# A recurrence's preparation of the next pair of heads, rearranged over the engines of one Trainium2 core

## The reference, cut to what matters

```python
xl = p_in + (shifted - p_in) * mu
r, k, v, xw, xa, xg = jnp.split(xl, RWKV_SPLITS, axis=-1)
w = -jax.nn.softplus(-(w0 + jnp.tanh(xw) @ w2)) - 0.5
decay = jnp.exp(-jnp.exp(w.astype(jnp.float32)))
a = jax.nn.sigmoid(a0 + xa @ a2)
kk = k * k_k
kk = kk / jnp.maximum(jnp.sqrt(jnp.sum(kk * kk, axis=-1, keepdims=True)), 1e-12)
k = k * (1.0 + (a - 1.0) * k_a)
# per token, with a_t = -kk and b_t = kk * a
sa = jnp.einsum('bhij,bhj->bhi', state, a_t)
state = state * w_t[:, :, None, :] + sa[..., None] * b_t[:, :, None, :] + v_t[..., None] * k_t[:, :, None, :]
y_t = jnp.einsum('bhij,bhj->bhi', state, r_t)
# behind the scan: group norm of y, then
y = y + jnp.sum(r * k * r_k, axis=-1, keepdims=True) * v
```

## Time and profile before

| | us |
|---|---|
| median of 3 runs | 2117.4 (2117.34 to 2122.9) |
| the profiled execution's own time | 2115.69 |
| its span, first to last instruction | 2113.9 |
| PE busy | 1930.1 (91%) |
| DVE, ACT, POOL busy | 875.9, 443.6, 1275.4 |
| mean granted clock of PE | 0.952 |

### The profile page before, as it was taken

The page is one execution under the profiler, slowest core; times in us unless marked ns, Lnnn a source line. Parts: engine busy times, 40 slices in busy tenths (PEclk is TensorE's granted clock), DMA queues, the critical chain, the costliest instruction groups (busy, mean ns, idle before and its releaser), DMA issues.

```text
span 2113.9 us, 29843 instructions
## 1 busy us (share of the span) xinstructions
PE 1930.1 (91%) x11700; PEld 1500.4 (71%) x11700; DVE 875.9 (41%) x1440; ACT 443.6 (21%) x876; POOL 1275.4 (60%) x615
## 2 busy tenths in 40 slices
PE   7999999878989999998899999967667899999998
PEld 5888888656658888886677766655565678888887
DVE  4333311468553333212223344384546735555301
ACT  3000000313430000001222356325423021112100
POOL 6888877553348888777465432351132667777773
PEclk9999999989989999999999999988876999999999
DMA  4222233211012222333323421310022223223231
GB/s 146 98 89 98 88 91 91 99 53 47 31 60 90 89 99 88 91 92 112 148 85 125 155 67 44 130 36 2 3 107 90 70 82 98 90 91 96 87 96 58
DMA packets 58780, 180.33 MB, mean 85 GB/s; under 512 B 6931, under 2 KB 13843, under 8 KB 58172
## 3 DMA queue, kind: packets, MB, share of 16 engines
q1 hardware_dynamic: 49132, 165.83, 23.5%
q10 hardware_dynamic: 9552, 13.13, 1.7%
HBM read 165.81 MB, written 13.13 MB: 85 GB/s over the span
## 4 chain that ended last, share of the span: by engine, by line
PE 80%; DVE 14%; ACT 3%; issue 2%; DMA 0%; ACTq 0%; POOL 0%; DVEq 0%; SPq 0%; POOLq 0%
PE bank L522 23%; PE bank L523 22%; PE bank L524 22%; PE bank L884 1%; PE bank L572 1%; PE bank L837 1%; DVE h_lo L1619 1%; PE bank L870 1%; DVE sq L2154 1%; PE bank L801 1%; DVE m_lo L2155 1%; PE bank L1040 1%; DVE xT L1666 1%; DVE tmp L1663 1%; DVE sq L2151 1%
## 5 line engine op out<-in xcount | busy, mean ns | idle before, releaser
L442 POOL TENSOR_TENSOR w_hi<-w_raw,one 128x1024 fp32r<-128x1024 f32 (+1 forms) x279 | 527.4, 1890 | 610.1 <-PE bank L524 600.1
L444 POOL TENSOR_TENSOR w_lo<-w_raw,w_hi 128x1024 fp32r<-128x1024 f32 (+1 forms) x279 | 698.9, 2505 | 21.9
L522 PE MATMUL bank<-h_hi,w_hi 128*128 128x512 f32 x1528 | 629.8, 412 | 25.1 <-DVE h_lo L1619 12.5
L523 PE MATMUL bank<-h_lo,w_hi 128*128 128x512 f32 x1528 | 608.8, 398 | 0.0
L524 PE MATMUL bank<-h_hi,w_lo 128*128 128x512 f32 x1528 | 608.5, 398 | 0.0
L522 PEld LDWEIGHTS bank<-h_hi,w_hi 128*128 128x128 f32 x1528 | 289.9, 190 | 119.2 <-issue 29.2
L523 PEld LDWEIGHTS bank<-h_lo,w_hi 128*128 128x128 f32 x1528 | 290.1, 190 | 76.6 <-issue 9.8
L524 PEld LDWEIGHTS bank<-h_hi,w_lo 128*128 128x128 f32 x1528 | 289.8, 190 | 70.8
L522 PE MATMUL bank<-a_hi,w_hi 128*128 128x512 f32 x528 | 209.3, 396 | 0.0
L523 PE MATMUL bank<-a_lo,w_hi 128*128 128x512 f32 x528 | 209.3, 396 | 0.0
L524 PE MATMUL bank<-a_hi,w_lo 128*128 128x512 f32 x528 | 209.3, 396 | 0.0
(11 more groups left out here) (345 smaller groups left out, 2177.6 us busy)
## 6 DMA issues: line engine op xcount, KB each, us to landing
w_raw<-w_ffn_gu_dram SPq DMA_DIRECT2D x88, 512.0 KB, 3.4
w_raw<-w_conv_up_dram SPq DMA_DIRECT2D x44, 512.0 KB, 3.5
w_raw<-w_ffn_down_dram SPq DMA_DIRECT2D x32, 448.0 KB, 3.2
w_raw<-w_ffn_down_dram SPq DMA_DIRECT2D x16, 512.0 KB, 3.5
w_raw<-w_out_dram SPq DMA_DIRECT2D x16, 512.0 KB, 3.5
w_raw<-w_gates_dram SPq DMA_DIRECT2D x16, 512.0 KB, 3.5
w_raw<-w_rwkv_dram SPq DMA_DIRECT2D x14, 512.0 KB, 3.5
w_raw<-w_conv_down_dram SPq DMA_DIRECT2D x16, 448.0 KB, 3.3
```

What stands on the lines that cost most here:

```text
L442: nc.gpsimd.tensor_tensor(w_hi[:, s, 0:width], raw, one[:, 0:1].to_broadcast([P, width]), ALU.mult).then_inc(sem("w_rounded"), 1)
L444: nc.gpsimd.tensor_tensor(w_lo[:, s, 0:width], raw, w_hi[:, s, 0:width].bitcast(F32), ALU.subtract).then_inc(sem("w_split"), 1)
L522: nc.tensor.matmul(dst, hi, rhs_hi[:, k, :], start=start and k == k0, stop=False)
L523: nc.tensor.matmul(dst, hi, rhs_lo[:, k, :], start=False, stop=False)
```

## The change

Nothing of the result is meant to change. The parts are:
- All four pairs' sigmoids are made ahead of pair 0 and kept (`sig`), in two pairs of PSUM banks by turns; one table with logarithm and exponential is loaded behind them (`logs()`).
- `decay` is a tile of 1 + 64 columns per chunk whose first column is 1: the exponential of `CUM` is written to columns 1 to 64 (`UPTO`), and columns 0 to 63 are `PREV`. The subtraction L2017 and one exponential go.
- ACT makes the key's factor (an Identity with scale and bias) and squares `pin` with a scale, which takes two operations from DVE. `KK` comes from `pin` in one operation with the norm.
- The product of `RATE` and `INV` moves from DVE to POOL, behind the masks of level 4.
- The head sums of the next pair move ahead of level 1 on PE; ACT and DVE have one or two operations of the preparation behind each level.
- A pair's turns stand between its scores, not ahead of the chunk terms of the pair before.
- Six of the 14 mixings move behind levels 1 to 3 of pairs 0 and 1; keys and squares are made two pairs ahead.
- POOL's splits of the first four merge chunks move behind its masks of pair 3.

```diff
-            KK0, MOD0, SG, RATE, CUM, UPTO = (scope.enter_context(nc.sbuf_tensor(n, [P, S], F32))
-                                            for n in ("KK0", "MOD0", "SG", "RATE", "CUM", "UPTO"))
+            KK0, MOD0, SG0, CUM = (scope.enter_context(nc.sbuf_tensor(n, [P, S], F32))
+                                   for n in ("KK0", "MOD0", "SG0", "CUM"))
+            decay = scope.enter_context(nc.sbuf_tensor("decay", [P, NCH, 1 + C], F32))
...
-            stream(FIRST["merge"], RING)
-
+
+            def rate_over_decay(m):
+                pool.wait_ge(*nth("decays", 2 * (m + 1)))
+                nc.gpsimd.tensor_tensor(RATE[m], RATE[m], INV[:, :], ALU.mult).then_inc(sem("rate_over_decay"), 1)
+
+            rate_over_decay(0)
...
+                    if k == 4 and m < 3:
+                        rate_over_decay(m + 1)
+            stream(FIRST["merge"], RING)
...
-            for step in range(1, 6):
-                fill(2 if step < 3 else 1)
-                rw_prepare(0, step)
+            fill(3)
+            pe.wait_ge(*nth("lora_in", 1))
+            for m in range(4):
+                lora(m)
+            pe.wait_ge(*nth("lora_read", 4))
+            fill(1)
+            head_sums(0)
+            fill(3)
...
-                level_start(m, 1)
+                if m < 3:
+                    pe.wait_ge(*nth("rw_tok", 4 * m + 4))
+                    head_sums(m + 1)
                 for k in range(1, 6):
                     level_x(m, k, 0)
                     if k > 1:
                         level_dt(m, k - 1, 1)
+                    else:
+                        level_start(m, 1)
...
-                    if m < 3:
-                        rw_prepare(m + 1, k + 1)
+                    if k == 1 and m < 3:
+                        key_norm(m + 1)
+                    elif k == 2 and m < 3:
+                        decays(m + 1)
+                    elif k == 4 and m < 2:
+                        key_rates(m + 2)
...
-            for j in range(14):
+            nc.vector.tensor_scalar(keep[:, :], prm[:, COL["k_a"]:COL["k_a"] + 4], -1.0, 1.0, ALU.mult, ALU.add)\
+                .then_inc(sem("keep_ready"), 1)
+            for j in range(5):
                 mix(j)
-                if j in PREPARE_AT:
-                    rw_prepare(0, PREPARE_AT[j])
+            nc.vector.memset(decay[:, :, 0:1], 1.0)
+            decay_sum(0)
+            keys(0)
+            mix(5)
+            decayed(0)
+            mix(6)
+            sums_out(0)
+            mix(7)
+            removal(0)
+            replacement(0)
+            keys(1)
...
-                    if m < 3:
-                        rw_prepare(m + 1, k + 1)
+                    if m < 2 and k < 4:
+                        mix(7 + 3 * m + k)
+                    if m < 3 and k < 5:
+                        (sums_out, decay_sum, decayed, removal)[k - 1](m + 1)
                 level_dt_out(m, 5)
+                if m < 3:
+                    replacement(m + 1)
+                if m < 2:
+                    keys(m + 2)
```

More of the change, by code:

```diff
@@ L1502, in _ @@
             nc.scalar.activation(pin[0:64, 12, :], pin[0:64, 12, :], ACT.Tanh).then_inc(sem("lora_in"), 1)
-            for step in range(1, 6):
-                rw_prepare(0, step)
-                fill_out((1, 1, 1, 1, 3)[step - 1])
+            fill_out(1)
+            for m in range(4):
+                sigmoids(m)
+            logs()
+            key_rates(0)
+            decays(0)
+            fill_out(1)
+            key_norm(0)
+            fill_out(3)
+            key_rates(1)
             flat = lambda x: x.rearrange("p a b -> p (a b)")
```

182 lines of the change are left out of this document (82 added, 100 removed).

## The result

The changed kernel takes 2065.05 us (median of 4 runs, 2061.17 to 2069.39) against 2118.43 (median of 4, 2117.34 to 2122.9): ratio 0.9745, 95% interval 0.972 to 0.977. That is 13 us under the 2078 of the forecast and just above the low end of its range, 2064. The profiled execution took 2061.17 us (span 2059.4), 54.5 less than the profiled one of before.

The account below looks back on a forecast made before the run. Latency of the recurrence's chain round PE, ACT and DVE was taken as the bound. Gains of 11.5 (start) and 32.8 (pairs) less 4.5 (walk), 39.8 us, took 2115.7 to 2075.9; 1.7 for the median made 2078, range 2064 to 2097.

Parts of the forecast that it names:

- The pool and its source: Recurrence, pairs 0 to 2: preparing the next pair costs 16 us a pair, 47 us in all, which the change can draw on.
- Start of pair 0: Ahead of pair 0: fewer mixings and no merge splits let its first mask product start at 1397.0, gain 11.5 us (9 to 13).
- The floor: Recurrence: a pair without preparation would take 28.7 us, from pair 3's 27.02 plus 1.68 to the next mask product.
- Front: Front of each pair: head sums between the two halves of the start add 1.0 us in pairs 0 to 2, 0.5 in pair 3.
- Levels: Levels of the pairs: DVE's added mixings and operations on sums cost 5.0 us in pairs 0 and 1, 1.3 in pair 2.
- Tables: Inside the pairs: no table loads left, against four per pair of 1.28 us; part of the 16 us, no separate term.
- The walk: Behind the recurrence: POOL's moved merge splits meet DVE's state products and add 4.5 us (0 to 9).
- All hidden: Rival: gains of 40.2 in the recurrence and 13 at pair 0's start, walk free; 2064, centred at 2066 us; chance 0.12.
- DVE's levels are worse: Rival, levels of the pairs: POOL's masks and the mixings collide, recurrence gains only 20.2, giving 2090 us; chance 0.24.
- The preparation still ends last: Rival, pairs: the product of rate and decay comes 10 us late in each, next scores wait; about 2112 us; chance 0.03.
- The lowered clock: Rival, all four pairs: PE runs at the low 1.2 GHz, 46.7 us a pair with the step, giving 2135 us; chance 0.03.

## Why the prediction was right, and where it was short

**The pool and its source.** Right. The preparation was what made pairs 0 to 2 long, and most of it came off: their excess over a pair without was 16 us and is 5.0, 5.9 and 1.7 (31.52, 32.47 and 28.27 less 25.22 + 1.32).

**Start of pair 0.** Forecast −11.5, measured −11.7 from the common split on (56.64 to 44.96). The chain was the one named: the last late copy, one ACT operation, two DVE products, with DVE idle before them. The reason was half right: I had the six moved mixings and the four splits as two gains that add. With the new code the mixings put back cost nothing, the splits put back 2.0 us, and both together 11.0; it was the pair of them that held DVE. The joint table had no part in it (56.54 us with it in the kernel before). And the estimate that DVE would be done at 1385 passed over what follows from it: with PE's late products ending last, DVE had room for all fourteen mixings.

**The floor.** This is the term that was mis-sized. "A pair without preparation would take 28.7 us" took pair 3 of the kernel before as it stood; in the changed kernel it is 25.22 + 1.32 = 26.5. That error enters all four pairs and makes 8 to 9 of the 10.4 us by which the recurrence came out shorter (117.48, forecast 127.9). The 1.80 us of pair 3 split as the runs show them: pauses of PE, 2.09 in that profile and 1.39 in this, 0.70; clock, 0.8 to 0.9 (the same code took 24.93 at 0.94 and 24.06 at 1.00, and 25.24 at 0.87 in the run with idle products, all without pauses); the order of products the rest, 0.2 to 0.3. The other 0.36 is the shorter step from the chunk terms. And the pauses hardly come in pairs 0 to 2 (0.37, 0 and 0.15 us), so their tails are shorter than pair 3's. I had the clock only as a rival that makes things worse, and wrote that the change makes pairs denser, without carrying it into the sum: 0.77 to 0.81 became 0.95 to 1.00. The run with idle products shows what it is worth, 2.5 us behind one wait of pair 1.

**Front.** Forecast +1.0 for pairs 0 to 2. The first read of X is at 5.95, 6.39 and 6.36 us after the first mask product, 5.26 in pair 3: +0.7, +1.1 and +1.1, as the head sums were to cost. Against the row that the term was added to, 6.42 in pair 3 before, they are −0.5, 0 and −0.1, since half 0's first product now stands ahead of the start of half 1; half 1's first read, which was to come 1 us later, comes 0.2 to 0.7 us later than its 7.75 there. The +0.5 for pair 3 did not come.

**Levels.** Forecast 0.9, 2.0, 2.1 and 0 in pair 0. From half 0's read in one level to the next: 5.25, 3.57, 5.58 and 2.38 us, in pair 3 4.60, 2.10, 2.34 and 2.63: +0.7, +1.5, +3.2 and −0.3. The prediction's 0.9 for level 1 has no working behind it: 1.26 + 3.0 = 4.3 us is less than the 4.55 of the row, so nothing should stick out. The sum of 5.1 against 5.0 is right by luck in its parts: level 3 lost 2 us to POOL, a collision that I had left to the rival. I had put POOL's product under level 5 and the chunk terms; but the masks of level 4 wait in the code only for the product of level 2, so it ran as soon as ACT had the decay, at 1411.22, in the middle of level 3. DVE was busy 3.53 of 3.57 us in level 2 and 5.54 of 5.58 in level 3, as predicted; the run with the mixings ahead takes 4.0 and 4.6 us off the pairs. Pair 2: +1.6 against 1.3, and 1.4 of it in level 3, where the same collision is.

**Tables.** None inside the pairs, as the order said. The joint load is worth 3.1 to 3.4 us per pair to the kernel before, and 2.8 in pair 2 of the changed one; the start of pair 0 gains nothing by it.

**The walk.** Forecast +4.5, measured +4.0, by the mechanism named: state products of 0.42 us grow to 2.2 each in the first step and one of 1.42 in the second, and come back as the splits are moved away. The Trainium skill's rule (SBUF — State Buffer, Who interferes with whom) fits here and ahead of pair 0: operations of two SBUF inputs took up to 2.88 us, about the length of the split's instruction beside them (2.72 to 2.78), while PSUM reads kept their 0.69.

**The rivals.** "All hidden" (2064 to 2066) gave the nearest time but not for its reason: neither were the levels hidden nor the walk free. "DVE's levels are worse" had its mechanism in level 3 and not its size. "The preparation still ends last" did not come; 10 us in three pairs would have been 2108, not the 2112 written. The lowered clock, which was to end slower, went the other way; the runs show it as a real force all the same, where a late DVE leaves PE idle ahead of pair 0 (0.50 there, and 30.79 us instead of 27.54).

## What to carry to other kernels

A floor read from one stage of a slow kernel carries that kernel's clock and its pauses: take the pauses out, note the granted clock beside it, and scale what PE does when the change closes its waits. Background work cost nothing here only where the engine beside it was idle or read PSUM; six mixings went for nothing into a hole of 12.55 us, and cost nearly their full length behind the levels. Two loads on DVE and POOL that cost 0 and 2.0 us alone cost 11.0 together: test them as a pair. And compare times inside a profile from a common row: starts that looked 2.0 and 2.8 us apart were the same to 0.1 us.

## What the runs showed of the hardware

- Extra products on PE that nobody reads made a kernel faster, 0.9973 (0.9963 to 0.9982), by holding the granted clock at 1.00 through a wait.
- The same code of pair 0 took 27.54 us behind a busy PE, at a clock of 1.00, and 30.79 behind one that had been idle for over 4 us, at 0.86.
- PE paused for 1.4 to 4.4 us in pair 3 with nothing recorded that it waited for, in the runs of the changed kernel and its variants. Pairs 0 to 2 had 0 to 1.8 us of it. The profile doesn't name the cause and it stays open.
- The version with the mixings ahead, the product on DVE and a split at the end of each pair takes 0.9698 (0.9684 to 0.9712) of the kernel before, and beats the changed kernel's 0.9745 by about 10 us.
